# Two transformer blocks on one core: the last feed-forward layer's up-projection by seven block products in place of eight

## The reference, cut to what matters

```
h2 = rmsnorm_2(x, norm_mlp_g[l])
up = jnp.square(jax.nn.relu(jnp.einsum('bsd,df->bsf', h2, w_up[l])))
x = x + jnp.einsum('bsf,fd->bsd', up, w_down[l])
```

## Time and profile before

| | |
|---|---|
| executions | 995.89, 996.32, 996.40 us |
| span of the profiled execution, first to last instruction | 994.1 us |
| TensorE matmul busy | 987.6 us, 4608 matmuls |
| VectorE busy | 682.7 us |
| ScalarE busy | 553.6 us |
| GpSimd busy | 118.6 us, 109 instructions |
| granted TensorE clock | 1.000 of full speed |

### The profile page before, as it was taken

How to read it: one execution, slowest core, us unless ns; L and a number is a source line. 1 busy time by engine, 2 the same in 40 slices (tenths; PEclk the granted TensorE clock), 3 DMA queues, 4 the chain that set the end, 5 groups by cost and what they waited for, 6 DMA issues and landing times.

```text
span 994.1 us, 12539 instructions
## 1 busy us (share of the span) xinstructions
PE 987.6 (99%) x4608; PEld 810.6 (82%) x4608; DVE 682.7 (69%) x998; ACT 553.6 (56%) x761; POOL 118.6 (12%) x109
## 2 busy tenths in 40 slices
PE   8999999999999999999999999999999999999998
PEld 7788888888777788888888888888888888888887
DVE  6666566668987667656565678776689767656663
ACT  7444343577665546444444586868885555443542
POOL 0000000022300000000000041169904000000000
PEclk9999999999999999999999999999999999999999
DMA  7987776586444546766666487658555546777761
GB/s 263 284 266 255 234 250 211 193 305 196 140 152 143 169 130 214 227 198 214 211 204 226 156 229 237 176 163 212 151 191 196 202 156 204 228 223 227 226 198 43
DMA packets 165465, 201.44 MB, mean 203 GB/s; under 512 B 55969, under 2 KB 111658, under 8 KB 165290
## 3 DMA queue, kind: packets, MB, share of 16 engines
q1 hardware_dynamic: 164826, 200.69, 64.3%
q10 hardware_dynamic: 592, 0.14, 0.1%
HBM read 182.45 MB, written 5.77 MB: 189 GB/s over the span
## 4 chain that ended last, share of the span: by engine, by line
PE 96%; DVE 2%; ACT 1%; POOL 1%; issue 0%; ACTq 0%; POOLq 0%; DVEq 0%
PE bank L1969 23%; PE bank L1971 23%; PE bank L1970 23%; PE bank L2087 7%; PE bank L2086 7%; PE bank L2085 7%; PE bank L1984 1%; PE bank L2136 1%; PE bank L2251 1%; DVE lo L1348 0%; PE bank L2151 0%; PE bank L2138 0%; PE bank L2374 0%; PE bank L2375 0%; PE bank L2347 0%
## 5 line engine op out<-in xcount | busy, mean ns | idle before, releaser
L1969 PE MATMUL bank<-hi,xh 128*128 128x512 f32 (+1 forms) x944 | 374.8, 397 | 0.9 <-DVE lo L1574 0.8
L1971 PE MATMUL bank<-hi,xl 128*128 128x512 f32 (+1 forms) x944 | 367.2, 389 | 0.0
L1970 PE MATMUL bank<-lo,xh 128*128 128x512 f32 (+1 forms) x944 | 366.5, 388 | 0.0
L1331 DVE TENSOR_TENSOR lo<-raw,hi 128x2048 fp32r<-128x2048 f32 (+1 forms) x111 | 253.9, 2289 | 146.2 <-ACT hi L824 146.2
L824 ACT ACTIVATE hi<-raw 128x2048 fp32r<-128x2048 f32 (+1 forms) x114 | 216.5, 1901 | 133.7 <-PE bank L2087 97.0
L1969 PEld LDWEIGHTS bank<-hi,xh 128*128 128x128 f32 x944 | 177.3, 188 | 39.7 <-issue 2.5
L1971 PEld LDWEIGHTS bank<-hi,xl 128*128 128x128 f32 x944 | 177.2, 188 | 37.2
L1970 PEld LDWEIGHTS bank<-lo,xh 128*128 128x128 f32 x944 | 177.5, 188 | 34.4
L1348 DVE TENSOR_TENSOR lo<-raw,hi 128x1024 fp32r<-128x1024 f32 (+1 forms) x108 | 131.9, 1230 | 43.1 <-ACT hi L833 42.4
L2085 PE MATMUL bank<-hi,hh 128*128 128x512 f32 (+1 forms) x306 | 119.3, 390 | 0.0
L2087 PE MATMUL bank<-hi,hl 128*128 128x512 f32 (+1 forms) x306 | 118.7, 388 | 0.0
(11 more groups left out here) (271 smaller groups left out, 961.6 us busy)
## 6 DMA issues: line engine op xcount, KB each, us to landing
raw<-in_w_in SPq DMA_DIRECT2D x48, 1024.0 KB
raw<-in_ffn_w_gu SPq DMA_DIRECT2D x82, 512.0 KB
raw<-in_ffn_w_down SPq DMA_DIRECT2D x22, 1024.0 KB
raw<-in_w_up SPq DMA_DIRECT2D x16, 1024.0 KB
raw<-in_w_down SPq DMA_DIRECT2D x16, 1024.0 KB
raw<-in_w_out SPq DMA_DIRECT2D x8, 1024.0 KB
distance_table<-ftab SPq DMA_DIRECT2D x8, 576.0 KB
raw<-in_w_proj_attn SPq DMA_DIRECT2D x4, 1024.0 KB
```

Source lines behind the costliest of these rows:

```text
L1331: nc.vector.tensor_tensor(lo[s][:, :, 0:width], raw[s][:, :, 0:width], hi[s][:, :, 0:width].bitcast(F32), ALU.subtract).then_inc(lo_done, 1)
L1969: nc.tensor.matmul(o, sh, wh, start=first and j == 0, stop=False)
L1970: nc.tensor.matmul(o, sh, wl, start=False, stop=False)
L1971: ins = nc.tensor.matmul(o, sl, wh, start=False, stop=last and j == 3)
```

## The change: what it does

The up-projection was 32 block products (2 token tiles x 2 row halves x 8 chunks), each one `portion`. Chunks 0 and 1 stay as they were. The six chunks 2 to 7 are taken in three pairs (`NPAIR = 3`). In a pair the product of a 2 x 2 block matrix of activations (token tile x row half) with a 2 x 2 block matrix of weights (row half x chunk) is made from 7 block products in place of 8 (Winograd's form of Strassen's scheme). For this

- four of the seven right-hand operands are sums of weight blocks. GpSimd makes them (`weight_sums`, L936: `tensor_tensor` on 128 x 2048 float32, both inputs in SBUF), in new tiles `operand`, which SP loads by `last_operand` (L623) ahead of the units' order;
- four left-hand operands are sums of activation blocks; GpSimd makes them once (L963 to L971) in `xn`, ScalarE and VectorE split them (`sum_h`, `sum_l`);
- each of the seven operands is a unit of its own, used for one token tile alone (12 matmuls in place of 24), so a pair has 7 + 4 = 11 units to be split by ScalarE and VectorE, where two chunks had 8;
- partial results are kept and added (`keep` on ScalarE, `add_product` on VectorE), and products p4, p6, p7 and p3 run on in a bank that holds an earlier result (`onto=True`);
- the square moves to ScalarE for these six chunks, and the last chunk's hidden values go through the DMA transposes like the others, in place of 8 transposes on TensorE (L2009).

The order of the units in a pair is p1, p2, a0, p6, a1, p7, p5, p4, b0, p3, b1, where a0, a1, b0, b1 are down units of the two chunks before. Semaphores of the earlier feed-forward layers and attention stages are shared between stages (renamed), which moves no instruction of theirs. The core of the diff:

```
+PRODUCTS = ["p1", "p2", "a0", "p6", "a1", "p7", "p5", "p4", "b0", "p3", "b1"]
+OPERAND = {"p1": 0, "p2": 1, "p6": 5, "p7": 2, "p5": 4, "p4": 1, "p3": 3}
+SUM_OF = {"p6": 2, "p7": 3, "p5": 1, "p4": 4}
...
+            def last_operand(j, b):
+
+                half, chunk = b % 2, 2 + 2 * j + b // 2
+                if j == 0:
+                    sp_eng.wait_ge(k_rl, 2)
+                else:
+                    sp_eng.wait_ge(lo_done, product_unit(j - 1, ("p1", "p4", "p7", "p3")[b]) + 1)
+                    sp_eng.wait_ge(last.t_made, 4 * j - (3, 0, 1, 1)[b])
+                src = col_view(a["w_up_2"])[:, 4 * half:4 * half + 4, chunk * W:chunk * W + W]
+                sp_eng.dma_start(operand[b][:, :, :], src).then_inc(last.b_in[b], 16)
...
                     columns(a["w_proj_attn_2" if c < 2 else "w_proj_rnn_2"], U_P2 + 2 * c + half, c % 2 * W, half)
+                    if (c, half) in ((2, 1), (3, 1)):
+                        last_operand(0, 2 * (c - 2))
...
+            for j in range(NPAIR):
+                i = 2 + 2 * j
+                if j < NPAIR - 1:
+                    last_operand(j + 1, 0)
+                last_down(i - 1, 1)
+                last_down(i, 0)
+                flip_last(i, 0, 2 * i + 1)
+                if j < NPAIR - 1:
+                    last_operand(j + 1, 2)
+                    last_operand(j + 1, 1)
+                last_down(i, 1)
+                flip_last(i, 1, 2 * i + 2)
+                if j < NPAIR - 1:
+                    last_operand(j + 1, 3)
+                last_down(i + 1, 0)
+                flip_last(i + 1, 1, 2 * i + 3)
+                flip_last(i + 1, 0, 2 * i + 4)
...
+            def weight_sums(j, which):
+
+                def sum_up(t, left, right, op):
+                    pool.wait_ge(last.t_made, 4 * j + t - 1)
+                    nc.gpsimd.tensor_tensor(operand[(4, 5, 2, 1)[t - 1]][:, :, :], operand[left][:, :, :],
+                                            operand[right][:, :, :], op).then_inc(last.t_made, 1)
+
+                for t in which:
+                    if t == 1:
+                        pool.wait_ge(last.b_in[0], 16 * j + 16)
+                        pool.wait_ge(last.b_in[2], 16 * j + 16)
+                        if j >= 1:
+                            pool.wait_ge(lo_done, product_unit(j - 1, "p5") + 1)
+                        sum_up(1, 2, 0, ALU.subtract)
+                    if t == 2:
+                        pool.wait_ge(last.b_in[3], 16 * j + 16)
+                        if j >= 1:
+                            pool.wait_ge(lo_done, product_unit(j - 1, "p6") + 1)
+                        sum_up(2, 3, 4, ALU.subtract)
+                    if t == 3:
+                        sum_up(3, 3, 2, ALU.subtract)
+                    if t == 4:
+                        pool.wait_ge(last.b_in[1], 16 * j + 16)
+                        pool.wait_ge(lo_done, product_unit(j, "p2") + 1)
+                        sum_up(4, 1, 5, ALU.subtract)
+
+            weight_sums(0, (1, 2, 3))
             norm_rstd(4)
...
+            weight_sums(0, (4,))
+            for j in range(1, NPAIR):
+                weight_sums(j, (1, 2, 3, 4))
...
+            def keep(j, k):
+
+                act.wait_ge(used, product_unit(j, ("p1", "p6", "p7")[k]) + 1)
+                if j == 0 and k == 0:
+                    act.wait_ge(last.s_lo, 4)
...
+                for j in range(NPAIR):
+                    last_split_lo(product_unit(j, "a0"))
+                    add_product(j, 0)
+                    last_split_lo(product_unit(j, "p6"))
+                    last_split_lo(product_unit(j, "a1"))
+                    last_merge(2 * j + 1)
+                    pair_planes(j, 0)
+                    last_split_lo(product_unit(j, "p7"))
+                    last_lo(2 * j + 1)
+                    last_split_lo(product_unit(j, "p5"))
+                    last_split_lo(product_unit(j, "p4"))
+                    last_split_lo(product_unit(j, "b0"))
+                    add_product(j, 1)
+                    last_split_lo(product_unit(j, "p3"))
+                    pair_planes(j, 1)
+                    last_split_lo(product_unit(j, "b1"))
+                    last_merge(2 * j + 2)
+                    last_split_lo(product_unit(j, "b1") + 1)
+                    add_product(j, 2)
+                    pair_planes(j, 2)
+                    last_split_lo(product_unit(j, "b1") + 2)
+                    pair_planes(j, 3)
+                    last_lo(2 * j + 2)
```

More of the change, by code:

```diff
@@ L922, in ffn_iter @@
                 split_hi(n + 4, off)
-                for b in range(f.banks):
-                    split_hi(n + 5 + b, off)
+                split_hi(n + 5, off)
             def ffn(f, width=lambda n: W):
@@ L1426, in ffn_iter @@
                 split_lo(n + 4, off)
[L1427 to L1428 removed]
+                split_lo(n + 5, off)
             def ffn(f, width=lambda n: W, after_first=None):
@@ new lines, in last_ffn @@
+            def last_ffn():
+                ffn_first(last)
+                second_chunk()
+                for j in range(NPAIR):
+                    for name in PRODUCTS:
+                        if name in OPERAND:
+                            product(j, name)
+                        else:
+                            last_down(2 * j + "ab".index(name[0]), int(name[1]))
+                for i in (NF2 - 2, NF2 - 1):
+                    for b in range(2):
+                        last_down(i, b)
```

752 lines of the change are left out of this document (496 added, 256 removed).

## The result

The changed kernel takes 1050.86 us (median of 4 executions, 1050.33 to 1051.79) where the kernel before takes 996.21: 1.0551 times as long, 95% interval 1.0536 to 1.0566. That is 54.7 us more; 33 were forecast, and the time lies 9 us outside the range. The span went from 994.1 to 1049.9 us, +55.8.

A forecast was written before the change was run, and what follows sets the result against it. TensorE's matmuls were taken as the bound, 987.6 of 994.1 us. Terms -9.1 + 3.4 + 3.3 + 8.4 + 25.0 + 1.7 = +32.7 gave 1026.8 us, with the median 2.2 above the span 1029 us; range 1005 to 1042.

The forecast's parts named there:

- the walk: Timeline of one pair's instructions across the engines: 53.1 us from a0 to a0, 40.8 of work and 12.5 of stalls.
- What is taken away: TensorE in the up-projection and last chunk: 36 matmuls (8.2 us) and eight transposes (0.9 us) fewer, together -9.1 us.
- What a sum costs: GpSimd's 2048-column weight sum: 4.5 us duration, VectorE held out for 4.3 us of it.
- port work: Shared SBUF port, per pair: VectorE's 32.0 us plus four sums of 4.3 held, 49.2 us against TensorE's 40.8.
- Start of the layer: Early operand load on SP's queue delays the third w_proj_rnn_2 unit near 780 us: 3.4 us lost.
- To the first a0: Before the first pair's down unit: activation sums delay p2's split, 3.3 us; sum 4 delays a0's split, 8.4 us.
- A pair: Sums delay VectorE's splits of p4, p2 and a0 by 1.6, 5.1 and 5.8 us: 12.5, in two pairs 25.0.
- Last pair and end: End of the layer: VectorE reaches `hl` 1.7 us late behind splits, adds and copies; no sum stalls in last pair.
- B: Rival: port shared piece by piece, so only the sum of work counts: +17.8 us, 1014 us; chance 0.15.
- C: Rival: the sums don't hold VectorE and splits are on time: -4.0 us, 992 us; chance 0.10.
- D: Rival: TensorE's clock falls too, each a0 at half pace behind stalls: 11.4 us on top, 1040 us; chance 0.15.

The follow-up runs named there:

- experiment 1: The changed kernel with all twelve weight sums cut to 16 columns, the six activation sums left whole: 1004.75 us, ratio 1.0084 to the kernel before.
- experiment 9: The changed kernel with all weight sums cut to 16 columns and the first operand load issued behind the last w_proj_rnn_2 unit: 997.23 us, ratio 1.0008.
- 12: The changed kernel with operand loads of a quarter of the bytes in pairs 2 and 3, plus identity transposes in TensorE's waits: 1042.41 us, ratio 1.046.
- experiment 5: The changed kernel with identity transposes into a free bank where TensorE sat idle, output unchanged: 1049.24 us, ratio 1.0526.

## Why the prediction was wrong, and what of it was right

The direction and the mechanism were right: a sum keeps VectorE's two-input work out for its whole length, at the places where the walk put it, and without the sums 46 of the 54.7 us are gone (experiment 1). The size was not. Step by step:

- **What is taken away, -9.1:** with nothing summed the span is 6.8 lower, and two waits of together 1.7 us are the rest but for 0.6. Right.
- **What a sum costs:** forecast 4.5 us alone and 4.3 held; measured 4.60 to 4.61 alone, 4.14 added to a split (6.43 for 2.29). Right. The port work of 49.2 us a pair is borne out by one pair in pieces, 49.3 us with VectorE idle for 0.8.
- **Start of the layer, +3.4: this step failed.** Up to the first ReLU 15.7 us were lost, 12.3 more than forecast. Two terms make them. The load's place in SP's queue was sized at 3.4 and is worth 6 to 8: with the late load 15.7 become 8.2, with tiny sums 7.1 become 0.8. It is more than the wait of 4.4 us, since the 12 matmuls behind that wait start over 4.2 us and not 2.5. The other term was put at nothing: "GpSimd's six sums ... start behind the norm's step" counts the sums behind the norm, but sums 1 to 3 stand ahead of it and run beside VectorE's `xn` products and splits of `w_out_2`. They are worth 7 to 9: 15.7 become 6.8 without them, and 8.2 become 0.8. TensorE waits 5.2 us for the products, the last of which stand behind the two stretched splits. With both mended 0.8 us are left (experiment 9), so this account is closed.
- **To the first a0, +3.3 and +8.4:** measured 11.3 for 11.7. Right in sum: waits of 2.8 and 6.6 us, and 1.3 that p2's matmuls lose at half clock.
- **A pair, +12.5 each: the second step that failed,** by 5.4 and 4.7 us. TensorE's waits came out well in sum, 11.3 for 12.5, but with luck: 3.1 before p4, 5.1 before p2 and 3.1 before a0 stand against 1.6, 5.1 and 5.8. From the split of p1 on, the walk holds: 20.0 us to the next a0 in both. The 5.6 us lie ahead of it. Counted from a0, p7's split ends at 12.2 and not 9.5; sum 1's operand takes 5.2 us and not 4.3 to land, beside other loads; so p4's split ends at 24.2 for 20.6, the halves at 31.0 for 26.3, and p1's split at 38.7 for 33.1. The walk took TensorE at full clock and the load as a lone one. p7's rounding waits for a0's matmuls, since they hold its slot, and these are 2.0 us late at half clock (1.7 in the next pair).
- **Which of these it is:** the 2.0 and 1.7 us of the slow a0 count in full, as far as the runs tell: the first pair of experiment 1 is longer than that of 9 by just what its a0 is slower, and so are the two pairs of 12 against each other, though no run sets the clock of a0 alone. Slow matmuls at p4 and p2 cost next to nothing (experiment 5). Smaller loads gave 7.2 us, but they also turn the order of sum 2 and p1's split around, so they are no measure of what the 0.9 us longer load did to the walk. How the remaining 3 to 4 us of a pair divide stays open.
- **Last pair and end, +1.7:** 2.9. The wait for `hl` is there, 0.9 us; the term left out the last a0 at half clock, 1.7 us.

The rivals. **B** (shared piece by piece) is refuted for one instruction, and what it would give was nearly made to happen with pieces: pairs of 49.4 and 49.3, as it said, at 1026.8 us for its 1014. The difference is the start again: the first a0 starts there 8.0 us before that of the changed kernel, which leaves 18.9 of the 27.0 us lost up to it, where B counted 8.4. **C** is refuted by every stretched row; with the weight sums cut its price of 992 was too low by 13: 3.7 for the early load beyond the 3.4 it had, 6.9 ahead of the first a0, where the sums over activations remain, and 3.0 for that a0 at half clock, less 0.4 at the end. **D** was right that the clock would fall behind stalls ("TensorE: Matmul & The Clock Gate", section "Why this matters for your kernels", not the one that the prediction names, in the Trainium skill says so of idle gaps, and the trace agrees: 0.67 where TensorE had idled, 1.00 where it had not), and wrong in its size: only part of an a0's matmuls are slow, so that it is 1.7 to 2.0 us longer and not 5.4. Three of them are 5.3 us for D's 11.4.

## What to carry to other kernels

Before moving elementwise work with two SBUF inputs to an idle GpSimd, add its whole duration to VectorE's and compare the sum with the bound engine's: here 32 us of port work a pair became 49, over TensorE's 40.8, and none of the orders tried saved that. Look at every place where such an instruction can run, also ahead of the stage that it serves, since here the stage ahead was the largest error. If the work must be there, cut it into short instructions: four of 512 columns in place of one of 2048 gave back 24 us, because no short VectorE step then waits for a whole sum. And ask what TensorE does behind each wait: in the changed kernel every wait before an a0 was paid for twice, once in the wait and again in slow matmuls.
